# Where the modulation's sums of a two-block transformer kernel are computed: between the steps of the first mixer, or on VectorE beside the MLP

## The reference, cut to what matters

```python
mod_shared = jax.nn.silu(c) @ w_mod + b_mod            # c: (1, 2048), w_mod: (2048, 12288)
mod = (mod_shared + mod_layer[l])[:, None, :]
shift1, scale1, gate1, shift2, scale2, gate2 = jnp.split(mod, N_MOD, axis=-1)
h = rms_norm(x, norm1_g[l]) * (1.0 + scale1) + shift1  # ... mixer ...
x = x + gate1 * (y @ w_out[l])
h = rms_norm(x, norm2_g[l]) * (1.0 + scale2) + shift2  # ... mixture of experts ...
x = x + gate2 * m
```

## Time and profile before

| what | value |
|---|---|
| median of 3 runs | 2847.93 us |
| the profiled execution | 2842.57 us |
| its span (first to last instruction) | 2840.9 us |
| mean granted TensorE clock | 0.908 |
| TensorE busy | 2426.5 us, 85% |
| VectorE busy | 1138.9 us, 40% |
| ScalarE busy | 813.1 us, 29% |
| bytes moved by DMA | 610.13 MB, mean 215 GB/s |

### The profile page before, as it was taken

How to read it: one execution, slowest core, us unless ns; L and a number is a source line. 1 busy time by engine, 2 the same in 40 slices (tenths; PEclk the granted TensorE clock), 3 DMA queues, 4 the chain that set the end, 5 groups by cost and what they waited for, 6 DMA issues and landing times. The chain is left out here.

```text
span 2840.9 us, 42405 instructions
## 1 busy us (share of the span) xinstructions
PE 2426.5 (85%) x18072; PEld 1890.0 (67%) x18072; DVE 1138.9 (40%) x1436; ACT 813.1 (29%) x1008; POOL 10.7 (0%) x56
## 2 busy tenths in 40 slices
PE   5998778987889879779999999996889477888885
PEld 5995558953777767479999989995774343443442
DVE  3763345535551520145555554554552311211112
ACT  3442313321221430244434344343440111111110
POOL 0000000000000000000000000000000000000000
PEclk9998988998896989889999999998999578999897
DMA  4446643457132432145555555552340479999998
GB/s 176 189 190 274 244 181 134 189 224 327 49 120 93 204 148 119 60 149 187 179 198 185 185 193 178 194 191 116 146 178 0 194 303 428 428 427 427 420 427 337
DMA packets 61370, 610.13 MB, mean 215 GB/s; under 512 B 8850, under 2 KB 9234, under 8 KB 16146
## 3 DMA queue, kind: packets, MB, share of 16 engines
q1 hardware_dynamic: 50114, 572.03, 50.5%
q0 software_dynamic: 1872, 23.07, 2.0%
q10 hardware_dynamic: 9216, 12.60, 1.2%
HBM read 674.76 MB, written 14.68 MB: 243 GB/s over the span
## 5 line engine op out<-in xcount | busy, mean ns | idle before, releaser
L1883 DVE TENSOR_TENSOR ffn_w_lo<-ffn_raw,ffn_w_hi 128x2048 fp32r<-128x2048 f32 x128 | 293.1, 2291 | 234.6 <-ACT ffn_w_hi L1876 234.6
L1876 ACT ACTIVATE ffn_w_hi<-ffn_raw 128x2048 fp32r<-128x2048 f32 x128 | 244.9, 1914 | 360.6 <-PE psum L1915 355.8
L1913 PE MATMUL psum<-u_hi,ffn_w_hi 128*128 128x256 f32 x1024 | 291.1, 284 | 15.1 <-DVE ffn_w_lo L1883 14.0
L2648 PE MATMUL psum<-moe_raw,moe_x_t 128*32 128x512 f32 x1536 | 219.0, 702 | 86.0 <-DMA moe_raw<-in_moe 78.5
L1914 PE MATMUL psum<-u_lo,ffn_w_hi 128*128 128x256 f32 x1024 | 290.8, 284 | 0.0
L1915 PE MATMUL psum<-u_hi,ffn_w_lo 128*128 128x256 f32 x1024 | 290.8, 284 | 0.0
L1913 PEld LDWEIGHTS psum<-u_hi,ffn_w_hi 128*128 128x128 f32 x1024 | 197.7, 193 | 16.0 <-DVE ffn_w_lo L1883 14.2
L1913 PE MATMUL psum<-ffn_w_hi,ffn_hid_hi 128*128 128x512 f32 x512 | 199.4, 389 | 0.0
L1914 PE MATMUL psum<-ffn_w_lo,ffn_hid_hi 128*128 128x512 f32 x512 | 199.4, 389 | 0.0
L1915 PE MATMUL psum<-ffn_w_hi,ffn_hid_lo 128*128 128x512 f32 x512 | 199.2, 389 | 0.0
L1914 PEld LDWEIGHTS psum<-u_lo,ffn_w_hi 128*128 128x128 f32 x1024 | 197.7, 193 | 0.5
(11 more groups left out here) (542 smaller groups left out, 4358.0 us busy)
## 6 DMA issues: line engine op xcount, KB each, us to landing
ring<-in_stream SPq DMA_DIRECT2D x107, 2048.0 KB, 10.9
moe_raw<-in_moe SPq DMA_DIRECT2D x96, 2048.0 KB, 17.9
ffn_raw<-in_ffn SPq DMA_DIRECT2D x128, 1024.0 KB, 4.8
moe_raw<-in_moe POOLq DMA_DIRECT2D x48, 2048.0 KB
expert_rows<-moe_stage ACTq DMA_DIRECT2D x192, 64.0 KB, 8.5
x<-in_x SPq DMA_DIRECT2D x2, 1024.0 KB, 8.1
mem<-in_mem SPq DMA_DIRECT2D x2, 1024.0 KB, 15.1
out<-x SPq DMA_DIRECT2D x2, 1024.0 KB, 4.9
```

What stands on the lines that cost most here:

```text
L1876: act.activation(self.w_hi[:, number % self.HIGHS], self.raw[:, number % self.RAWS], ACT.Copy)\
L1883: dve.tensor_tensor(self.w_lo[:, number % self.LOWS], self.raw[:, number % self.RAWS], self.w_hi[:, number % self.HIGHS].bitcast(F32), ALU ...
L1913: pe.matmul(out, lhs[0], rhs[0], start=start, stop=False)
L2648: mm = pe.matmul(summed(tile)[strip(q), :], e.x_t[:, tile // 4 % 2, UNIT_KC * u + c, strip(tile % 4)], w[:, c * COLS:(c + 1) * COLS], star ...
```

## The change

The sums leave the first mixer. All `Spot`s go, with `c_pad`, `take`, `turn`, `copy`, the 48 units of `w_mod` in the stream, and the stage `modulation`. The new `Modulation` lives in the MLP's scope:

- The weights come as 96 pieces of 1 MB: for each of the six sections (in the order shift1, scale1, shift2, scale2, gate1, gate2) 16 pieces of 128 rows by 2048 columns. SyncE loads them into 3 buffers behind the MLP's own loads.
- VectorE does `sums = sums + piece * silu(c)` per partition, one `scalar_tensor_tensor` of 128 by 2048 for each piece, at the end of the MLP's step `number`, in 4 of every 5 steps from step 4 on. The sums of a section stay spread over 128 partitions.
- GpSimd clears the sums of each section (6 memsets of 128 by 2048), and SyncE loads the two biases into two of their rows.
- Four sections are folded to columns on TensorE, each by 16 matmuls of 128 by 128 against a column of ones at the head of `up(e)` for e = 4, 6, 9 and 11; ScalarE copies the 16 columns out, and TensorE waits for that copy before it uses the rest of that bank.
- The two gate sections are folded and spread by 8 matmuls with a matrix of ones in `final_norm`, with 8 ScalarE copies behind the root. `silu(c)` is computed in the first block of `mlp`.

```diff
+    RAWS, BANK, COLUMN_SECTIONS, FOLDS = 3, 3, 4, (4, 6, 9, 11)
...
+    def load(self, sp, i):
+        if i >= self.RAWS:
+            sp.wait_ge(self.summed, i - self.RAWS + 1)
+        sp.dma_start(self.raw[:, i % self.RAWS], self.io["mod"][i]).then_inc(self.raw_in[i % self.RAWS], 16)
+
+    def loads_with(self, sp, number):
+
+        for i in range(self.RAWS, len(MOD_ORDER) * KC):
+            if 9 + (i - self.RAWS) * 5 // 4 == number:
+                self.load(sp, i)
+        for v in range(len(MOD_ORDER)):
+            if 6 + 20 * v == number:
+                sp.wait_ge(self.cleared, v + 1)
+                sp.dma_start(self.sums[0:2, v % 2, :], self.io["mod_bias"][v]).then_inc(self.bias_in, 16)
+
+    def clear(self, pool):
+        for v in range(len(MOD_ORDER)):
+            if v >= 2:
+                pool.wait_ge(self.folded, v - 1)
+            pool.memset(self.sums[:, v % 2, :], 0.0).then_inc(self.cleared, 1)
+
+    def sum_after(self, dve, number):
+
+        for i in range(len(MOD_ORDER) * KC):
+            if 4 + i * 5 // 4 == number:
+                v, c = i // KC, i % KC
+                if c == 0:
+                    dve.wait_ge(self.bias_in, 16 * (v + 1))
+                elif i:
+                    dve.wait_ge(self.summed, i)
+                dve.wait_ge(self.raw_in[i % self.RAWS], 16 * (i // self.RAWS + 1))
+                at = self.sums[:, v % 2, :]
+                dve.scalar_tensor_tensor(at, self.raw[:, i % self.RAWS], self.c_silu[:, c:c + 1], at, ALU.mult, ALU.add)\
+                   .then_inc(self.summed, 1)
+
+    def fold_with(self, pe, e):
+
+        for v in range(self.COLUMN_SECTIONS):
+            if self.FOLDS[v] == e:
+                pe.wait_ge(self.summed, KC * (v + 1))
+                for c in range(KC):
+                    mm = pe.matmul(bank(self.k, self.BANK)[:, T + c:T + c + 1], self.sums[:, v % 2, c * P:(c + 1) * P],
+                                   const(self.k, "ones")[:, 0:1], start=True, stop=True)
+                mm.then_inc(self.folded, 1)
...
+    def copy_after(self, act, number):
+
+        for v in range(self.COLUMN_SECTIONS):
+            if 4 + 8 * (self.FOLDS[v] - 1) + 2 == number:
+                act.wait_ge(self.folded, v + 1)
+                act.activation(self.cols[:, v * KC:(v + 1) * KC], bank(self.k, self.BANK)[:, T:T + KC], ACT.Copy)\
+                   .then_inc(self.copied, 1)
```

In `rwkv_prepare`, one of the six places (the others read alike):

```diff
-    spot = mod.spot(2, 5)
-    with nc.Block(no_gpsimd_drain=True) as block:
-        block.sync(spot.sync)
-        block.scalar(spot.scalar)
+    with nc.Block(no_gpsimd_drain=True) as block:
 
         @block.tensor
         def _(pe):
...
-            spot.tensor(pe)
```

In `mlp` and `final_norm`:

```diff
             act.activation(u_hi[:], u[:], ACT.Copy).then_inc(k.act_sem, 1)
+            act.activation(mod.c_silu[:], cols_of(k, "c"), ACT.Silu)
...
+            for i in range(mod.RAWS):
+                mod.load(sp, i)
             for number in range(f.RAWS, len(order)):
                 sp.wait_ge(f.low, number - f.RAWS + 1)
                 f.load(sp, number)
+                mod.loads_with(sp, number)
+
+        block.gpsimd(mod.clear)
...
                 f.split_low(dve, number)
+                mod.sum_after(dve, number)
...
+            for n in range(8):
+                act.wait_ge(k.mod_rows, n + 1)
+                act.activation(gates[:, n // 4, n % 4 * COLS:(n % 4 + 1) * COLS], bank(k, n), ACT.Copy)
```

More of the change, by code:

```diff
@@ L545 @@
 class Modulation:
[L551 to L632, removed]
-        spot = Spot(self, self.g, groups, b)
-        for _ in range(groups):
-            self.take_group()
-        return spot
-class Spot:
-    def __init__(self, mod, first, groups, b):
-        self.mod, self.groups, self.b = mod, range(first, first + groups), b
-    def sync(self, sp):
-        for g in self.groups:
-            self.mod.load_behind(sp, g)
-    def tensor(self, pe):
-        for g in self.groups:
-            if g:
-                self.mod.turn(pe, g - 1, self.b)
-                pe.wait_ge(self.mod.copied, g)
-            self.mod.product(pe, g, self.b)
-    def scalar(self, act):
-        for g in self.groups:
-            if g:
-                self.mod.copy(act, g - 1, self.b)
-            self.mod.take(act, g, self.b)
+    RAWS, BANK, COLUMN_SECTIONS, FOLDS = 3, 3, 4, (4, 6, 9, 11)
@@ L1063, in _ @@
                     load_unit(k, sp, i * 4 + first + SLOTS + j, (first + j) % SLOTS)
-            load_next(k, sp, lora, k.ft_done, f0 + 26)
+            for j in range(8, 11):
+                load_next(k, sp, first + j, k.ft_done, f0 + 4 * (j // 2 + 1))
         @block.tensor
@@ L1123, in rwkv_project, with rwkv_prepare @@
     k.pieces += 24
-def rwkv_prepare(nc, k, mod, mix, lora, AR, sig, neg, a, gate, kk, scratch, out):
+def rwkv_prepare(nc, k, mix, lora, AR, sig, neg, a, gate, kk, scratch, out):
     s = k.dve_steps
@@ L1319, in _, with rwkv_round @@
             s.settle()
-def rwkv_round(nc, k, mod, t, Xs, Ys, AR, B, K, v_tm, b_tms, k_tms, groups, Rs, Us, ys, tmps, state, gate, out):
+def rwkv_round(nc, k, t, Xs, Ys, AR, B, K, v_tm, b_tms, k_tms, groups, Rs, Us, ys, tmps, state, gate, out):
     s = k.dve_steps
@@ L1378, in rwkv_round @@
     invert(nc, k, Xs, groups)
-    group = [mod.take_group() for _ in range(2)]
     with nc.Block(no_gpsimd_drain=True) as block:
-        @block.sync
-        def _(sp):
-            for g in group:
-                mod.load_behind(sp, g)
         @block.tensor
@@ L1394, in _ @@
                 mm.then_inc(k.rw_r, 1)
-            mod.turn(pe, group[0] - 1, 6)
-            pe.wait_ge(mod.copied, group[0])
-            mod.product(pe, group[0], 6)
             for half in halves:
@@ L1419, in _ @@
             if not t:
-                pe.wait_ge(mod.out, group[0] + 1)
                 for half in halves:
@@ L1426, in _ @@
                     mm.then_inc(k.rw_state_mm, 1)
-            pe.wait_ge(k.rw_y_act, 4 * t + 2)
-            mod.turn(pe, group[1] - 1, 0)
-            pe.wait_ge(mod.copied, group[1])
-            mod.product(pe, group[1], 0)
             for half in halves:
@@ L1457, in _ @@
                .then_inc(k.rw_root, 1)
-            mod.take(act, group[1], 0)
         @block.vector
@@ L1924, in up @@
                     for m in range(4):
+                        if half == 0 and m == mod.BANK:
+                            mod.await_copy(pe, e)
                         for c in range(4):
@@ L2045, in _ @@
             sp.dma_start(weight[:], io["final_norm"]).then_inc(k.small_in, 16)
+        @block.tensor
+        def _(pe):
+            for n in range(8):
+                pe.matmul(bank(k, n), const(k, "ones"), gates[:, n // 4, n % 4 * COLS:(n % 4 + 1) * COLS], start=True,
+                          stop=True).then_inc(k.mod_rows, 1)
         @block.scalar
@@ L2933, in program @@
             mixed = sb("mixed", [P, 16, T], mixer)
-            mod = Modulation(k, mod_all, lambda n, shape: sb(n, shape, mixer), sem)
             u = sb("u", [P, KC, T], mixer)
```

181 lines of the change are left out of this document (44 added, 137 removed).

## The result

The changed kernel takes 2802.49 us (median of 4 runs, 2801.61 to 2806.29) against 2849.31 (4 runs, 2840.66 to 2850.72): a ratio of 0.9844, 95% interval 0.9822 to 0.9867, so 47 us less by medians. I had said 2780 (68 less than the median shown then). The forecast's own range was 2766 to 2796: the time lies 6.5 us above it, and only just inside the wider stretch, 2761 to 2804, to which I had given 8 of 10. By the profiled executions the span went from 2840.9 to 2804.6, 36.3 less, where the sum said 65.

The account below looks back on a forecast made before the run. Chains were taken to bound the mixer, TensorE the MLP, DMA the experts. From the profiled 2840.9 us, -93.1 - 12.0 + 20 + 20 = -65 gave 2775.8; the median was placed at 2780, range 2766 to 2796.

Parts of the forecast that it names:

- the sum: Whole kernel: all terms added to the profiled span of 2840.9 us, 65 us less, so 2775.8.
- What goes: Mixer: exposed time of the groups in the prepare blocks, tiles and rounds leaves, 93.1 us less.
- What the clock gives back: Mixer: without groups TensorE's bursts start cold and run slower, 20 us more, bounds 8 and 35.
- What the MLP pays on TensorE: MLP: four folds at 3.7 us each plus 1.3 for the clock behind, 20 us more, bounds 14.8 and 36.
- On VectorE and DMA: MLP: 96 sums fit VectorE's idle time (0 us, range 0 to 15); loads reach DMA share 0.85, 0 us.
- The margin of half a microsecond: MLP's hidden-block steps: VectorE's gathers, delayed by sums, still come 0.5 us before TensorE needs them, in 9 of 15 blocks.
- `modulation` and `final_norm`: Stage of 12.95 us goes whole, `final_norm` grows about 1.0: 12 us less, bounds 10 to 13.
- the clock takes more: Rival: mixer bursts stay cold, 35 us instead of 20, and folds cost 7 to 9 each; about 2800 us, chance 0.13.
- the lower bound of the clock's term: Mixer: least cost of cold starts, from line 1404 and the long stand alone, 8 us.

Follow-up runs that it names:

- run 3: Changed kernel with 16 matmuls of 128x512 on constants between the products of lines 1281 and 1291 in each recurrent round: 2793.57 us.
- run 5: Changed kernel with 6 matmuls of 128x512 on constants at the end of each inversion, deltanet tiles included: 2787.70 us.
- run 9: Changed kernel with 6 matmuls of 128x512 on constants behind the products of line 1281 in each round: 2788.19 us.
- run 10: Changed kernel with 2 matmuls of 128x512 on constants at the end of the two inversions of the rounds alone: 2790.48 us.
- run 2: Changed kernel without the MLP's four folds, their copies and TensorE's wait for them, the columns cleared instead: 2796.77 us.
- run 11: Changed kernel with matmuls on constants in the mixer's idle blocks and 6 behind the rounds' two inversions: 2773.68 us, ratio 0.9747 to the kernel before.
- run 7: Changed kernel with matmuls on constants in the mixer's idle blocks, behind each inversion and spread through round 1: 2777.24 us.

## Why the prediction was wrong

**What goes: right.** I matched every instruction that both kernels have and followed by how much it comes earlier. At the ends of eight blocks or groups the lead grows by 5.1, 2.6 and 13.1 us in `deltanet_prepare` (forecast 5.1, 2.8, 13.3), by 5.9, 13.9 and 6.9 in the last three changed blocks of `rwkv_prepare` (5.9, 14.1, 7.1), and by 8 us in each round at the first group (8.4, 7.7). So 63.5 of the 93.1 us are shown. In the other places a cold start falls into the same stretch, and I take them at the forecast.

**What the clock gives back: this step failed.** I put 20 with an upper bound of 35; it was 41. Removed (by the forecast) less net (measured), stretch by stretch:

| stretch | removed | net | given back | forecast |
|---|---|---|---|---|
| deltanet stages, to the start of `rwkv_prepare` | 38.1 | 27.8 | 10.3 | 7.4 |
| `rwkv_prepare` and the transposes | 34.6 | 23.2 | 11.4 | 6.3 |
| round 0 | 9.3 | -0.9 | 10.2 | 1.5 |
| round 1 and `mixer_out` | 11.2 | 1.8 | 9.4 | 4.7 |
| sum | 93.2 | 51.9 | 41.3 | 19.9 |

"Given back" is what is left of a subtraction, but the traces have it a second way. Without lines 609 and 620 TensorE is busy with the same instructions in both kernels, and this busy time grew from 246.8 to 255.7 us in the first stretch, from 34.6 to 48.1 in the second and from 179.2 to 199.2 in the two rounds: 42.4 in all. The part of it at a granted clock of 0.50 grew from 85 to 176 us.

The largest miss is round 0. I charged it 1.5 us for line 1404 and nothing for the products behind it, 9 us in the kernel before and 17 in the kernel after. They were warm in the trace, and I took that as their own nature. They were warm because the group stood ahead of them, just as the earlier trace rows show it for round 1, where I did charge the triples. Runs 3, 5, 9 and 10 show it: with 6 matmuls on constants 12.5 us come back in the rounds. The bound failed with the step, as it was made only of the steps that I had named. The second miss: lines 1166 and 1170 needed 7.0 more, not 2.5, because they run cold from their first record to their last; I let them recover.

Both misses point one way. The rule that I had quoted from the Trainium skill (TensorE: Matmul & The Clock Gate, HAM oscillation), that gaps between bursts put the array back to half clock again and again, would have given the upper bound, which was nearer. This trace agrees with it at lines 1093 and 1097, 7.2 us each behind a pause of 8.35. The stream of round 0, 0.50 for 13 busy microseconds, is a case that this rule of gaps doesn't cover.

**What the MLP pays on TensorE: right**, 18.7 (run 2) against 20, in the terms named: 3.5 us for the one-column matmuls and 1.2 for the clock behind them (3.7 and 1.3). **On VectorE and DMA: right**, 0.1 against 0. The margin of half a microsecond held; line 1870 never kept TensorE waiting. **`modulation` and `final_norm`: right**, -12.3 against -12. The drain of 1.38 us that the Trainium skill gives beside the table load (ScalarE: Activation LUTs, What ACT_TABLE_LOAD costs) doesn't show in this trace: the load begins 0.02 us behind ScalarE's last read, and the root 0.01 us behind the load.

**Cross attention** is 1.7 us longer, which no step had. Its TensorE work is the same, and it is the clock again: the 64 records of line 396 (398 before) take 29.33 us against 27.71, because the first 3 us of them run cold. Windows at their head, the kernel after and then the kernel before:

```profile
1115.10:1118.10 3.00, 3.00 (x4) 1.44 (x5) 0.00 (x0) 0.00 (x0) 0.00 (x0) 0.50 0.00 0
```

```profile
1166.90:1170.00 3.10, 3.10 (x9) 1.43 (x8) 0.00 (x0) 0.00 (x0) 0.00 (x0) 1.00 0.01 3
```

The stage took 148.4 in runs 5 and 9, 146.6 in run 11 and 150.1 in the others. TensorE is busy in it at 0.50 for 12.5 us, 8.5 us and 15.6 to 16.0 us in these three cases. Why the clock falls at another place in one kernel than in another isn't shown.

I had written that I was wrong if the mixer's stages shrink by under 60 us. They shrank by 51.9. The rival "the clock takes more" (2800) was the case that came true, by its mechanism and nearly by its time, though I had put 8 us of its excess on the folds, which cost what the forecast said.

Two slips in my sums change nothing: the removed times add up to 93.2, not 93.1, and the lower bound of the clock's term, 8, is 6.2 by the steps that I named for it.

## What to carry to other kernels

Work that fills a TensorE queue between thin products isn't only time that can be removed: it can be what keeps the clock up. When taking it out, go through everything that runs behind it until the next long pause and take it at half rate for the upper bound, not the next instruction alone. Where a stream of thin products follows a short pause, a few dense matmuls on resident data inside that pause, beside another engine's work, are worth a try: here two in each of two rounds took 10.6 us off them, six took 12.5 off, and the pauses grew by 0.7 and 2.4 us in all. Such matmuls spread through a stream that cools anyway were a loss of 5.4.

## What the runs showed of the hardware

- The granted clock has a memory. The same 32 products of 128x64 (64 records), TensorE fully busy, took 13 us at 0.50 where the stream had fallen cold near its start, and 7 us at 1.00 where it was warm; nothing in the stream itself brought it up for 13 us (the changed kernel) or down for 14 (run 10). Two matmuls of 128x512, 1.05 us, decided between the two.
- In triples with 64-row products the clock fell from 1.00 to 0.50 within 8 us, TensorE being busy all the while (run 3, round 1, from 830 to 838).
- The same instructions behind nearly the same pause came out at 3.72 us or at 7.19 (line 1110 in run 7, line 1111 in run 11). A difference of a few microseconds between kernels with such bursts may be nothing but this.
- A second stream of 1 MB loads took the DMA share of the MLP from 0.50 to 0.84 and left the first stream's landing at 5.1 us (4.8 before), with no wait for it.
